# Prompt attention of a hybrid decoder: when the branch weights are turned and copied, and how wide a score matmul is

## What is computed

```python
def nsa_attend(q, pos_q, kc, vc, gather_sel, n_blocks, kw, vw, pos_w, gates):
    qg = q.reshape(b, tq, NSA_KV_HEADS, NSA_GROUP, NSA_HEAD_DIM) * NSA_HEAD_DIM ** -0.5
    p_c = masked_softmax(jnp.einsum('bqghd,bcgd->bqghc', qg, kc), mask_c)
    o_c = jnp.einsum('bqghc,bcgd->bqghd', p_c, vc)
    ...
    p_s = masked_softmax(jnp.einsum('bqghd,bqgmd->bqghm', qg, k_s), mask_s)
    o_s = jnp.einsum('bqghm,bqgmd->bqghd', p_s, v_s)
    ...
    p_w = masked_softmax(jnp.einsum('bqghd,bkgd->bqghk', qg, kw), mask_w)
    o_w = jnp.einsum('bqghk,bkgd->bqghd', p_w, vw)
    o = gt[..., 0:1] * o_c + gt[..., 1:2] * o_s + gt[..., 2:3] * o_w
```

## Time and profile before

| | us |
|---|---|
| median of 3 runs | 2314.84 |
| lowest, highest | 2313.59, 2324.66 |
| the profiled execution | 2319.71 |
| its span | 2317.9 |
| PE busy in the span | 2113.2 (91%) |
| DVE, ACT busy | 857.8 (37%), 583.8 (25%) |
| granted PE clock, mean | 0.964 |

### The profile page before, as it was taken

The page is one execution under the profiler, slowest core; times in us unless marked ns, Lnnn a source line. Parts: engine busy times, 40 slices in busy tenths (PEclk is TensorE's granted clock), DMA queues, the critical chain, the costliest instruction groups (busy, mean ns, idle before and its releaser), DMA issues. The chain is left out here.

```text
span 2317.9 us, 37915 instructions
## 1 busy us (share of the span) xinstructions
PE 2113.2 (91%) x16201; PEld 1423.1 (61%) x16201; DVE 857.8 (37%) x2179; ACT 583.8 (25%) x1481; POOL 124.4 (5%) x128
## 2 busy tenths in 40 slices
PE   4799999999999999689999999869888999999998
PEld 2567666767676666556666666545566666666543
DVE  3154545444454545411366566624321000000111
ACT  2133222223232323200344454423352000000000
POOL 0000000001010101000000000012220000000000
PEclk9799999999999999889999999979998999999999
DMA  2200110101010100141100000098695311111011
GB/s 90 69 11 20 47 39 20 47 11 47 11 47 11 48 10 21 33 131 43 42 11 10 10 1 10 1 299 298 232 359 171 127 32 32 32 32 32 0 61 62
DMA packets 121584, 151.22 MB, mean 65 GB/s; under 512 B 27865, under 2 KB 105089, under 8 KB 112865
## 3 DMA queue, kind: packets, MB, share of 16 engines
q1 hardware_dynamic: 110724, 76.78, 11.9%
q0 software_dynamic: 10704, 72.16, 8.7%
HBM read 136.83 MB, written 16.26 MB: 66 GB/s over the span
## 5 line engine op out<-in xcount | busy, mean ns | idle before, releaser
L758 PE MATMUL g_ps<-hT,g_W 128*128 128x352 f32 x1536 | 527.6, 474 | 8.4 <-DMA g_W<-in_w_in_dram 8.4
L758 PEld LDWEIGHTS g_ps<-hT,g_W 128*128 128x128 f32 x1536 | 270.4, 192 | 116.4 <-issue 15.2
L2482 DVE SCALAR_TENSOR_TENSOR m_sg<-m_sg,m_ps 128x352 f32<-128x352 f32 x48 | 25.0, 521 | 360.6 <-PE m_ps L2422 360.6
L1500 PE MATMUL p_ps<-hT,Wpair 128*128 128x352 f32 x384 | 125.1, 465 | 0.6 <-PEq L1258 0.6
L2434 PE MATMUL m_ps<-m_Wo,m_mixed 128*128 128x512 f32 (+1 forms) x288 | 124.0, 592 | 1.4 <-DVE m_mixed L2485 1.4
L2448 ACT ACTIVATE m_sg<-m_ps 128x352 f32<-128x352 f32 x48 | 22.3, 465 | 386.6 <-PE m_ps L2415 386.6
L2415 PE MATMUL m_ps<-hT,Wgates 128*128 128x352 f32 x384 | 117.3, 464 | 1.6 <-DVEq L2471 1.6
L2415 PE MATMUL m_ps<-hT,m_Wgates 128*128 128x352 f32 x384 | 115.6, 459 | 0.0
L2415 PEld LDWEIGHTS m_ps<-hT,Wgates 128*128 128x128 f32 x384 | 73.8, 193 | 42.9 <-DVEq L2471 1.7
L2415 PEld LDWEIGHTS m_ps<-hT,m_Wgates 128*128 128x128 f32 x384 | 73.0, 190 | 40.6
L1911 PE MATMUL s_ps<-identity,s_G 128*128 128x128 f32 x512 | 75.3, 289 | 24.2 <-ACT s_XT L2126 20.0
(11 more groups left out here) (402 smaller groups left out, 3340.8 us busy)
## 6 DMA issues: line engine op xcount, KB each, us to landing
g_W<-in_w_in_dram SPq DMA_DIRECT2D x32, 512.0 KB, 4.8
n_x<-in_x_prompt_dram SPq DMA_DIRECT2D x8, 512.0 KB, 7.8
g_S<-in_state_gdn_dram SPq DMA_DIRECT2D x8, 512.0 KB, 4.2
out_dram<-g_S POOLq DMA_DIRECT2D x8, 512.0 KB, 3.8
Wpair<-in_w_in_dram SPq DMA_DIRECT2D x16, 256.0 KB, 3.9
Wgates<-in_w_in_dram SPq DMA_DIRECT2D x8, 512.0 KB, 5.3
m_Wgates<-in_w_in_dram SPq DMA_DIRECT2D x8, 512.0 KB, 5.2
m_Wo<-in_w_out_dram SPq DMA_DIRECT2D x1, 4096.0 KB, 15.2
```

What stands on the lines that cost most here:

```text
L758: ins = pe.matmul(ps[:, k.bank, 0:w], W[:, c_, kt, :], hT[:, kt, t0:t0 + w], start=kt == 0, stop=kt == KT - 1)
L1500: ins = pe.matmul(ps[:, fill_bank(n), 0:w], W[:, "qz".index(x), kt, :], hT[:, kt, t0:t0 + w], start=kt == 0, stop=kt == KT - 1)
```

## The change

1. PE: `turn_co` moves from even step m, behind `scores(m)`, to the end of odd step m-1, behind that step's turns and fills. `s_order` follows: the weights now come last among the users of `sT` in an odd step.
2. DVE: at even steps the copy to `cs` moves from behind `maxima(m)` to ahead of it. At odd steps `weights` moves from behind the copy of the first group to ahead of `maxima(m)`.
3. PE: of a step's fills two stay between the first and the second group of turns; the third and fourth move behind the second group.
4. PE: score pieces are at most 256 columns wide instead of 512, for S and for W. The choice between S and W is by columns issued, as before.

```diff
-    CMP = 5 * P
+    CMP, PIECE = 5 * P, 2 * P
...
-                    slc = [(s_slc[:, k0:min(k0 + 512, w)], q, g.slcT[rows, k0:min(k0 + 512, w)])
-                           for k0 in range(0, w, 512)]
+                    slc = [(s_slc[:, k0:min(k0 + PIECE, w)], q, g.slcT[rows, k0:min(k0 + PIECE, w)])
+                           for k0 in range(0, w, PIECE)]
...
-                    win = [(s_win[:, k0:min(k0 + 512, w)], q, g.winT[rows, w0 + k0:w0 + min(k0 + 512, w)])
-                           for k0 in range(0, w, 512)]
+                    win = [(s_win[:, k0:min(k0 + PIECE, w)], q, g.winT[rows, w0 + k0:w0 + min(k0 + PIECE, w)])
+                           for k0 in range(0, w, PIECE)]
...
                 if m % 2 == 0 and 0 <= j < J:
-                    turn_co(j)
                     values_win(j)
...
                     if a == 0:
-                        for n, kt in fill_at[m]:
+                        for n, kt in fill_at[m][:2]:
                             fill(n, kt)
+                for n, kt in fill_at[m][2:]:
+                    fill(n, kt)
+                j = (m - 3) // 2
+                if m % 2 and 0 <= j < J:
+                    turn_co(j)
...
             for m in range(STEPS):
-                maxima(m)
-                slc = slc_groups(m - 1) if 0 <= m - 1 < U else []
                 j = (m - 4) // 2
                 if m % 2 == 0 and 0 <= j < J:
                     v.wait_ge(s_full, s_order["co", j] + 1)
                     v.tensor_copy(cs[:], sT[:, 0:3 * P]).then_inc(s_free, 1)
-                if slc:
-                    turn_out(m - 1, 0)
-                if m % 2 == 0 and 0 <= j < J:
-                    output(j)
                 j = (m - 3) // 2
                 if m % 2 and 0 <= j < J:
                     weights(j)
+                maxima(m)
+                slc = slc_groups(m - 1) if 0 <= m - 1 < U else []
+                if slc:
+                    turn_out(m - 1, 0)
+                j = (m - 4) // 2
+                if m % 2 == 0 and 0 <= j < J:
+                    output(j)
                 if len(slc) > 1:
                     turn_out(m - 1, 1)
```

More of the change, by code:

```diff
@@ L2533, in prompt_plan @@
     for m in range(steps):
-        j = (m - 4) // 2
-        if m % 2 == 0 and 0 <= j < len(units) // 2:
-            s_order["co", j] = len(s_order)
         if 0 <= m - 1 < len(units):
@@ L2539, in prompt_plan @@
                 s_order["slc", m - 1, a] = len(s_order)
+        j = (m - 3) // 2
+        if m % 2 and 0 <= j < len(units) // 2:
+            s_order["co", j] = len(s_order)
         if 0 <= m - 2 < len(units):
```

## The result

| | before | after |
|---|---|---|
| median, us (20 runs each) | 2321.77 | 2311.36 |
| the profiled execution's span, us | 2317.9 | 2307.5 |
| the stage, first score matmul to the modelled end of the last values matmul, us | 378.5 | 367.5 |

The ratio after to before is 0.9961, with a 95% interval of 0.9951 to 0.9972: 9 us less of about 2321; the two medians are 10.4 us apart, and so are the two spans. The forecast was 7.7 us less. The stage in the two traces is shorter by 11.0 us. The forecast time of 2307.1 us started from a median of three runs, 2314.84; that of 20 runs lies 7 us higher, so the change is what is to be compared, not the time.

A forecast was written before the change was run, and what follows sets the result against it. PE's list and its waits were taken to bound the stage. Terms -14.4 + 4.7 + 1.0 - 0.7 + 1.0 + 0.7 = -7.7 us took the median 2314.84 to 2307.1 us, range 2297 to 2319.

The forecast's parts named there:

- -14.4 us of waits: PE's waits in `turn_slc` for DVE's copy to `cs`, by starts, all to go: -14.4 us.
- `turn_co` moved, put at nothing: Its three transposes on PE cost 0.48 us, 32 times, before and after: nothing gained or lost.
- The second window group, +4.7: `turn_win(.., 1)` on PE newly waits for ACT's copy of the first window group out of `wT`: +4.7 us.
- `turn_co` waits for the last copy, 0.30 late in steps 13, 29, 45: At odd steps' end `turn_co` waits for DVE's last copy out of `sT`; step 57 gives 0.1: +1.0 us.
- The moved fill in step 15, -0.7: PE's 0.8 us wait at the head of step 16 for ACT's projection-fill copy is partly covered: -0.7 us.
- Steps 51 and 52: DVE is late; one 2.0 us PE idle replaces three summing to 2.1; most of step 52's 1.3 returns: +1.0 us.
- The last steps: Steps 61 to 66, without fills: ACT's copy holds step 62, gaining 0.3 instead of 1.1: +0.7 us.
- Pieces of 256: 224 more S and W matmul records on PE, their loads hidden: 0 us.
- the one in which nothing is late next: ACT's list starts earlier or copies are shorter, and the clock dip goes: -15.1 us, 2299.7; chance 0.20.
- the one in which the copy to `cs` stays late: DVE has not finished the odd step, eight 1.25 us operations: +4 us, 2311; chance 0.15 shared with rival 2.
- rival 3: In `scores`, loads of added pieces come outside: price 23 us, giving +15, 2330; chance 0.10, including a part of it.
- rival 2: Even steps' gains go to waits for ACT's copy and `turn_co`'s own: all 7.7 us lost, 2314.8; shared chance 0.15.

The follow-up runs named there:

- The run with fills ahead: Changed kernel with the third and fourth fill between the second `turn_slc` and second `turn_win` group; stage 361.6 us, ratio to before 0.9931.
- the two runs on pieces: Pieces of up to 512 columns in the changed kernel, ratio to before 0.9947; pieces of 256 alone in the kernel before, 0.9996.
- the run with ACT's copy early: Fills between the two second turn groups, pieces of 512, ACT copying the first window group right behind the exponential of S; stage 363.1 us, ratio 0.9923.

## Why the prediction was right, point by point

- *What bounds the stage.* Right: PE's list and its waits. The copy to `cs`, and only its place in DVE's list, released it. The two runs that differ in nothing else are 6.0 us apart in head 1.
- *-14.4 us of waits.* Right: the row is gone, and the even steps of qt 2 and 3, where nothing new waits, are 0.94 to 1.00 shorter (0.95 to 1.0 forecast).
- *`turn_co` moved, put at nothing.* This is the term that was mis-sized. Even steps without a wait lose 0.48 us (step 16: 7.58 to 7.11), but odd ones without a wait gain only 0.33 to 0.34 (step 19: 3.53 to 3.86). That is 0.15 us in up to 31 places, so some 4.6 us at most. In its old place `turn_co` stood between scores and values. Ahead of the first values matmul the weight load waited 0.17 us for nothing but its issue, and this row of the kernel before has all but vanished (1.3 us in 4 places above):

```profile
PEld p_ps L1582 <- issue: 5.2, 31, 0.2
```

  I took the 0.48 us from one row as the operation's price; it was the price of the operation in that place. Three transposes with others behind them take 0.33 us from start to start, 0.11 each (1201.85 in the earlier trace rows to the row below). The last two of the step, with S behind them (1202.49), take 0.31 instead of 0.22, so the step paid something at this border before the change too, and `turn_co` put there adds its 0.33 alone.

```profile
1202.18 0.38 PE L1553 MATMUL p_ps<-identity,p_Pw 128*128 128x128 f32 x2
```

  That the change of matmul shape causes the rest is argued from these rows and not shown by an experiment.
- *The second window group, +4.7.* Right in kind and nearly in size; wrong in the sign that I named for it. PE's own wait row has 3.4 us in 5 places, not 5 to 8 us in some 20: most of these waits lie under modelled ends, and only starts show them (the weight load's row has 31 places). By starts, the waits in head 1 are 0.17, 0.19, 0.10 and 0.22 in even steps (forecast 0.19, 0.18, 0.10, 0.22), 0.14, 0.22 and 0.05 in odd ones (0.24, 0.22, 0.04). The 0.46 more in step 10 did not come (5.66, as in step 26); why is not shown. The run with fills ahead won 4.2 us back. What I had not counted is that PE's next work behind such a wait also starts late: two transposes ahead of S take 0.37 us instead of 0.31 (steps 10 and 26).
- *`turn_co` waits for the last copy, 0.30 late in steps 13, 29, 45.* Step 29 went from 6.11 to 6.91; I had 6.89. The length is right by luck: by starts `turn_co` comes 0.68 us behind two transposes that take 0.22, so it is 0.46 late and not 0.30, and its own price is 0.33 and not 0.48. The row of these waits has steps 13, 29, 45 and 51; step 57 is not in it. Step 29, which answers to the earlier trace rows:

```profile
1282.69 0.44 PE L1553 MATMUL p_ps<-identity,p_Pw 128*128 128x128 f32 x2
1282.75 0.56 DVE L1693 COPY p_PTs<-p_ps 128x384 f32<-128x384 f32 x1 [1.26 <-PE p_ps L1543]
...
1283.37 0.55 PE L1560 MATMUL p_ps<-identity,p_cob 128*128 128x128 f32 x3 [0.24 <-DVE p_PTs L1693]
```

- *The moved fill in step 15, -0.7.* Nearly right: step 15 lost 0.15 us where step 31, the same but for this, gained 0.45.
- *`weights` at the head of odd steps, 0.* Right: between the two runs that differ in its place, the steps of qt 4 to 7 in heads 0 to 2 are alike to 0.02 us, and steps 7, 23 and 39 are 0.33 us longer where it stands behind the first copy.
- *Steps 51 and 52.* Right: one wait of 1.70 us (2.0 forecast) for the three of the earlier trace rows, with the dip still behind it.

```profile
1408.00 0.42 DVE L1693 COPY p_PTs<-p_ps 128x256 f32<-128x256 f32 x1
...
1408.48 0.55 PE L1560 MATMUL p_ps<-identity,p_cob 128*128 128x128 f32 x3 [1.70 <-DVE p_PTs L1693]
...
1411.66 3.07 PE L1500 MATMUL p_ps<-hT,Wpair 128*128 128x352 f32 x6
```

- *The last steps.* Step 62 lost 0.24 us (0.3 forecast), step 63 grew by 0.33 as written.
- *Pieces of 256.* Right to 0.35 us: scores of step 15 last 1.92 us, 1.91 before. The rule of the Trainium skill, TensorE: Matmul & The Clock Gate, section The mechanism, by which a load overlaps running matmuls only where the row group differs, does not hold here: 224 added loads, each shown as 0.18 us long, cost 0.35 us in all. The 60 cycles a matmul of its TensorEngine Tiling (Array Packing), section Instruction Overhead, are not seen either: 3.2 us by that estimate, 0.35 measured.

So the mechanism was right and the forecast 3.3 us short of the stage's 11.0. From step 3 to step 47 the traces give 8.1 us where the forecast's terms give 5.4. The odd steps are 2.95 us better than forecast: `turn_co`'s 0.15 in most of them, and 0.2 more in steps 17 and 33, where `values_slc` no longer waits. Step 10 is 0.5 better. The other even steps are 0.7 worse, which the late starts behind new waits and the pieces are about enough for. The rest, 0.6 us, lies in step 48 and after it.

Of the rivals, the one in which nothing is late next is refuted by the new waits, and the one of exposed loads by the two runs on pieces. The rival in which the wait only moves falls, as the stage is 11.0 us shorter, and so does the one in which the copy to `cs` stays late, as its row is gone. The upper end of the range was written as 2319 for a third of rival 3's price behind rival 2; with 23 us that sum gives 2322.5.

## What to carry to other kernels

Where one bank has several users, look at the engine that empties it, not at the one that fills it: the same move on PE alone cost 0.75%, and with one copy moved ahead in DVE's list it gained 0.5%. Then ask which copy is late next for each later user, and put independent work exactly between a fill of the bank and its next use; the fills did more there than at either end of the step. Price an operation that moves by the step lengths around it, since the same three transposes cost 0.48 us in one place and 0.33 in another.

## What the runs showed of the hardware

The dip of the granted clock to 0.50 (the lower level, 1.2 of 2.4 GHz) behind step 51 does not follow from the kernel's wait there. The changed kernel has it; the kernel with pieces of 512 has the same 1.7 us wait and none, and step 52 takes the same 4.05 us in three further kernels with a wait of 1.7 or 1.8 us. With all fills in the middle the wait is the same and the step takes 7.02. One execution of each kernel was profiled, so whether the dip differs from execution to execution of one kernel is not shown. Their windows (PE, PEld, DVE, ACT, POOL busy, PEclk, DMA share, GB/s), the first of the changed kernel, the second with 512:

```profile
1411.00:1413.00 2.00, 2.00 (x8) 1.49 (x7) 1.65 (x4) 1.43 (x7) 0.00 (x0) 0.50 0.00 0
```

```profile
1404.00:1414.00 10.00, 8.30 (x67) 5.53 (x64) 8.62 (x31) 5.21 (x21) 0.00 (x0) 1.00 0.01 3
```

The dip is worth 1.65 us in step 52, and one in the last step of the run with ACT's copy early 3.0, which is as much as several of the effects above. Without the step lengths the stage totals would have misled: they put the pieces of 512 at 2.0 us where 0.35 is theirs.
